# Feed work moved behind a quad's copies, and a stage's last operand pair ahead of its weights

## The reference

```python
x = x + 0.5 * swiglu(rmsnorm(x, ffn1_norm[l]), ...)      # (silu(h @ w_gate) * (h @ w_up)) @ w_down, D_FF = 2816
x = x + mixer(rmsnorm(x, mix_norm[l]))                    # layer 0: gated short convolution, layer 1: attention
x = x + 0.5 * swiglu(rmsnorm(x, ffn2_norm[l]), ...)
...
y = rmsnorm(x, final_norm)
```

## Time and profile before

| | us |
|---|---|
| median of 3 timed runs | 2286.36 (2285.08 to 2289.76) |
| the profiled execution | 2290.18 |
| its span | 2288.4 |
| TensorE busy | 2206.6 |
| VectorE busy | 1372.1 |
| ScalarE busy | 843.4 |
| GpSimd busy | 191.8 |

### The profile page before, as it was taken

One profiled execution on the slowest core, in us unless ns is written; L12 is line 12 of the kernel. 1 busy time (PEld: TensorE's weight loads), 2 busy tenths in 40 slices (PEclk: granted clock), 3 DMA queues, 4 the chain that ended last, 5 costly groups with the idle time before them and its releaser, 6 DMA issues.

```text
span 2288.4 us, 37348 instructions
## 1 busy us (share of the span) xinstructions
PE 2206.6 (96%) x16008; PEld 2132.4 (93%) x16008; DVE 1372.1 (60%) x1861; ACT 843.4 (37%) x1325; POOL 191.8 (8%) x213
## 2 busy tenths in 40 slices
PE   8999999899999999998999999899999999999995
PEld 8999999899899999998999999887787899999995
DVE  6565656755765657467465655855555455756556
ACT  5242424422432434234243332534333332424233
POOL 1000001100110000002000000210000110000002
PEclk9999999999999999999999999999999999999998
DMA  6244343232342343432433342322222142343422
GB/s 195 74 106 116 93 134 97 77 113 83 88 125 79 102 121 87 134 89 69 138 98 112 96 134 74 88 88 74 75 74 75 55 128 82 98 121 87 135 73 75
DMA packets 92917, 226.70 MB, mean 99 GB/s; under 512 B 11024, under 2 KB 25664, under 8 KB 92752
## 3 DMA queue, kind: packets, MB, share of 16 engines
q1 hardware_dynamic: 71712, 186.35, 26.1%
q0 software_dynamic: 17152, 30.26, 7.4%
q10 hardware_dynamic: 3888, 7.70, 0.9%
HBM read 217.17 MB, written 7.09 MB: 98 GB/s over the span
## 4 chain that ended last, share of the span: by engine, by line
PE 86%; DVE 10%; ACT 2%; DMA 1%; issue 1%; POOL 0%; DVEq 0%; ACTq 0%
PE ps L1068 65%; PE ps L1209 15%; DVE w_lo L790 3%; PE ps L1145 2%; PE ps L1127 2%; ACT w_hi L555 1%; DVE xg_lo L803 1%; PE ps L1113 1%; DVE w_quad L797 1%; DVE x L933 1%; DMA w_raw<-w 1%; DVE hop_lo L814 1%; DVE x L928 1%; DVE x L920 1%; DVE w_lo L787 0%
## 5 line engine op out<-in xcount | busy, mean ns | idle before, releaser
L1068 PE MATMUL ps<-xg_hi,w_hi 128*128 128x288 f32 x3584 | 777.2, 298 | 13.2 <-DVE w_lo L787 8.6
L1068 PE MATMUL ps<-xg_hi,w_lo 128*128 128x288 f32 x3584 | 765.4, 295 | 0.0
L1068 PE MATMUL ps<-xg_lo,w_hi 128*128 128x288 f32 x3584 | 764.6, 295 | 0.0
L1068 PEld LDWEIGHTS ps<-xg_hi,w_hi 128*128 128x128 f32 x3584 | 574.5, 189 | 44.8 <-issue 26.5
L1068 PEld LDWEIGHTS ps<-xg_lo,w_hi 128*128 128x128 f32 x3584 | 576.0, 189 | 0.0
L1068 PEld LDWEIGHTS ps<-xg_hi,w_lo 128*128 128x128 f32 x3584 | 575.8, 188 | 0.0
L541 ACT ACTIVATE w_hi<-w_raw 128x1024 fp32r<-128x1024 f32 x232 | 245.3, 1058 | 658.0 <-PE ps L1068 617.1
L1209 PE MATMUL ps<-hop_hi,w_hi 128*128 128x288 f32 x1344 | 406.5, 302 | 47.2 <-ACT snap L694 31.4
L898 DVE TENSOR_TENSOR scaled<-ps,rstd 128x576 f32<-128x576 f32 x176 | 133.1, 757 | 467.1 <-PE ps L1068 466.7
L1209 PE MATMUL ps<-hop_lo,w_hi 128*128 128x288 f32 x1344 | 404.0, 301 | 0.0
L1209 PE MATMUL ps<-hop_hi,w_lo 128*128 128x288 f32 x1344 | 403.3, 300 | 0.0
(11 more groups left out here) (108 smaller groups left out, 1505.9 us busy)
## 6 DMA issues: line engine op xcount, KB each, us to landing
w_raw<-w SPq DMA_DIRECT2D x232, 512.0 KB, 3.5
w_quad<-q SPq DMA_DIRECT2D x180, 256.0 KB, 3.9
w_quad<-q POOLq DMA_DIRECT2D x72, 256.0 KB, 6.1
w_quad<-q SPq DMA_DIRECT2D x80, 192.0 KB, 3.1
w_quad<-q POOLq DMA_DIRECT2D x32, 192.0 KB, 5.0
x<-x_t ACTq DMA_DIRECT2D x8, 288.0 KB, 6.9
k_t<-k_sb ACTq DMA_DIRECT2D x8, 288.0 KB, 2.1
v_t<-v_sb ACTq DMA_DIRECT2D x8, 288.0 KB, 2.5
```

The lines of the kernel that those rows point to most:

```text
L1068: mm = pe.matmul(ps[:, 2 * it.slot + b, 0:HALF], wt[:, r, cols], xt[:, k, b * HALF:(b + 1) * HALF], start=(i == 0 and n == 0), stop=(i == ...
```

## The change

Four things are moved; no arithmetic is added or left out.

1. In a feeding phase ScalarE's and VectorE's feed work of a quad's first tile goes behind the last copy and g4's weights, and that of its second tile into the next quad, behind g1. Only in the phase's last quad (`ends`) the feed work stays where it ends the quad, and `xg_lo` of the first tile goes ahead of line 928.
2. At the last tile of an up phase or of `conv_in`, VectorE rounds the pair (`pair_parts`) ahead of the weights instead of behind them.
3. g4 of a phase's first quad is prepared at the last but one tile, behind g2, instead of at the last one, behind g3; the order of the counted steps follows.
4. `attn_out` calls the same helper `feed`; its order does not change.

GpSimd's sums of squares and all loads stay as they are.

```diff
-        for part in ("g1", "g2", "g3", "g4") if it.phase.quads else ("tile",):
+        if not it.phase.quads:
+            parts = ("tile",)
+        else:
+            parts = ("g1", "g2", "g3", "g4") if it.u else ("g1", "g2", "g4", "g3")
+        for part in parts:
...
-            if nxt is not None and nxt.phase.quads:
-                it.ahead.append(nxt.steps["g4"])
+            if it.u == it.phase.n - 2 and it.phase.after.quads:
+                it.ahead.append(it.phase.after.items[0].steps["g4"])
...
                     act.activation(snap[:, 3, :], ps[:, bank_b, 0:HALF], ACT.Copy).then_inc(snapped, 1)
                     split_hi(g1)
+                    if p.feeds is not None and it.u:
+                        feed(p, before, 1)
                     act.wait_ge(tile_done, it.done + P6)
                     act.activation(snap[:, 1, :], ps[:, bank_a, 0:HALF], ACT.Copy).then_inc(snapped, 1)
                     split_hi(g2)
                     split_hi(g3)
-                    if p.feeds is not None:
-                        act.wait_ge(tile_read, it.evicted + 1)
-                        if p.feeds < N_NORM - 1:
-                            xg_upper(p.feeds, first)
+                    ends = p.feeds is not None and it.u == QUADS - 1
+                    if ends:
+                        feed_upper(p, it, 0)
                     act.wait_ge(tile_done, it.done + P7)
                     act.activation(snap[:, 2, :], ps[:, bank_a, 0:HALF], ACT.Copy).then_inc(snapped, 1)
-                    if p.feeds is not None:
-                        squares(p.feeds, first)
-                        act.wait_ge(tile_read, it.evicted + 2)
-                        if p.feeds < N_NORM - 1:
-                            xg_upper(p.feeds, second)
-                        elif it.u == 0:
-                            act.preload_act_table(ACT.Sqrt)
-                        squares(p.feeds, second)
                     split_hi(g4)
+                    if ends:
+                        squares(p.feeds, 2 * it.u)
+                        feed(p, it, 1)
+                    elif p.feeds is not None:
+                        feed(p, it, 0)
+
+            def feed_upper(p, it, second):
+
+                act.wait_ge(tile_read, it.evicted + 1 + second)
+                if p.feeds < N_NORM - 1:
+                    xg_upper(p.feeds, 2 * it.u + second)
+                elif it.u == 0 and second == 0:
+                    act.preload_act_table(ACT.Sqrt)
+
+            def feed(p, it, second):
+                feed_upper(p, it, second)
+                squares(p.feeds, 2 * it.u + second)
...
+                    last = it.u == p.n - 1
+                    if last:
+                        pair_parts(p, j)
                     if not (p.norm is not None and it.u == 0):
                         for w in it.ahead:
                             split_lo(w)
-                    if it.u % 2:
+                    if it.u % 2 and not last:
                         pair_parts(p, j)
...
                     split_lo(g1)
+                    if p.feeds is not None and it.u:
+                        feed(p, 2 * it.u - 1)
                     split_lo(g2)
...
                     split_lo(g3)
+                    if ends and p.feeds < N_NORM - 1:
+                        norm_lo(p.feeds, 2 * it.u)
                     dve.wait_ge(snapped, shots + 4)
                     dve.scalar_tensor_tensor(halves(x[:, m2, :]), banks(it.slot + 1), -share, halves(x[:, m2, :]),
                                              ALU.mult, ALU.add).then_inc(x_part, 1)
-                    if p.feeds is not None and p.feeds < N_NORM - 1:
-                        norm_lo(p.feeds, 2 * it.u)
                     dve.wait_ge(x_part, 2 * it.quad + 2)
                     dve.scalar_tensor_tensor(halves(x[:, m2, :]), snap[:, 2:4, :], -share, halves(x[:, m2, :]),
                                              ALU.mult, ALU.add).then_inc(tile_read, 1)
-                    if p.feeds is not None and p.feeds < N_NORM - 1:
-                        norm_lo(p.feeds, 2 * it.u + 1)
                     split_lo(g4)
+                    if ends:
+                        feed(p, 2 * it.u + 1)
+                    elif p.feeds is not None:
+                        feed(p, 2 * it.u)
```

More of the change, by code:

```diff
@@ L686, in quads @@
                     g1, g2, g3, g4 = it.ahead
-                    first, second = 2 * it.u, 2 * it.u + 1
                     bank_b, bank_a = 2 * it.slot + 1, 2 * it.slot + 3
@@ L934, in quads, with feed @@
                                              ALU.mult, ALU.add).then_inc(tile_read, 1)
-                    if p.feeds is not None and p.feeds < N_NORM - 1:
-                        norm_lo(p.feeds, 2 * it.u + 1)
                     split_lo(g4)
+                    if ends:
+                        feed(p, 2 * it.u + 1)
+                    elif p.feeds is not None:
+                        feed(p, 2 * it.u)
+            def feed(p, i):
+                if p.feeds < N_NORM - 1:
+                    norm_lo(p.feeds, i)
             def attn_out(p):
@@ L946, in attn_out @@
                         split_lo(w)
-                    norm_lo(p.feeds, it.u)
+                    feed(p, it.u)
             def conv(p):
@@ L991, in conv @@
                             pair_sums(p, jj)
+                            last = it.u == p.n - 1
+                            if last:
+                                pair_parts(p, jj)
                             for w in it.ahead:
                                 split_lo(w)
-                            pair_parts(p, jj)
+                            if not last:
+                                pair_parts(p, jj)
             def qkv(p, t):
```

## The result

The changed kernel takes 2248.1 us (median of 4 runs, 2246.9 to 2249.0), the kernel before 2285.9 us (4 runs, 2285.1 to 2289.8): a ratio of 0.983, interval [0.981, 0.985], 37.8 us less. The forecast was 2238 us, 48.2 us less, in a range of 2217 to 2260. The profiled execution took 2248.87 us with a span of 2247.0; it lies 0.8 us above its median, that of before 4.2 us above its own. Between the two profiles there are 41.3 us.

What follows compares the result with a forecast made beforehand. TensorE, busy 96%, was taken to lose time only to waits, mainly for a VectorE-ScalarE loop in feeding stages, and lowered clock. Waits 36.2 plus clock 12.0 gave 48.2 us off 2286.4: 2238 us, range 2217 to 2260.

Steps and rivals of the forecast that it cites:

- the loop: VectorE and ScalarE work repeated each quad of a feeding stage: 63.0 us to become 53.0, against TensorE's 50.1.
- the waits for `xg_lo`: TensorE's waits, mostly in the next stage's first tile: to grow from 1.0 to near 2.9 us a stage.
- half clock: TensorE at 1.2 instead of 2.4 GHz behind waits: loss to fall from 18.0 to 6.0 us.
- the targeted waits: TensorE's waits for `snap` copies, `hop_lo` and `xg_lo`: 51.8 us to become 15.6, gain 36.2.
- the second turn: Second quad's pass in a feeding stage, from line 933 to line 933: 16.15 us to become 13.2.
- rival C: One more sum holds each turn in feeding stages: 2257 us, chance 0.16; sign: line 933 every 14 us.
- the loads priced at nothing: Loads waiting for g3 start 2.0 us later; block ready at 19 us, wanted at 22.3: no cost.
- Part 2: Stage ends: last pair rounded ahead of the weights, g4 one tile earlier; `hop_lo` waits of 15.8 us fall to 4.0.
- Rival D: Copies late for another reason, loop keeps its 15 us, only stage-start gains come: 2270 us, chance 0.03.
- part 1: Feeding stages: feed work moved behind the copies, taking 2.05 us a turn off ScalarE's chain and 1.8 off VectorE's.
- three-pair starts: Four stage starts: three small waits, about 1.0 us together, instead of 1.76 each; should not lower the clock.
- The first turn: Feeding stage's start to the first line 933's end: 16.1 us to become 15.1.

Runs made afterwards that it cites:

- part 1 alone: Changed kernel with the last pair again rounded behind the weights and g4 back at the last tile, only feed work moved: 2249.6 us.
- g3 between: Changed kernel with the last pair's first part rounded ahead of g3's weights and its second part behind them: 2237.9 us.
- g1 first: Changed kernel with ScalarE rounding the next quad's g1 ahead of the second copy: 2241.1 us.
- small sums: Changed kernel with GpSimd's first sum of squares replaced by a constant fill, the others adding 8 of 576 columns: 2218.3 us.

## Why the prediction was right, and where its size was off

**Right.** The direction, the mechanism and the places. The copies' waits of up to 4.7 us are gone, the loop is what bounds a feeding stage, and the waits for `xg_lo` grew to 2.3 to 2.5 us a stage where 2.9 were forecast, each with a half clock of 3.4 us behind. At the stage starts four waits of 0.4 and four of 0.2 us are left, and the nine with four pairs went. The clock gave 12.2 us where 12.0 were forecast; that all four waits for `xg_lo` lower it is in part luck, since in other kernels two or three of four did.

**Off: the feeding stages' waits.** This is where the size was lost: 22.1 us of the targeted waits are left, not 15.6. In four stages 4 x 2.9 = 11.6 us were forecast; measured are 9.8 for `xg_lo` and 6.4 for copies, 16.2 together. In the fifth stage, whose waits were to go, 1.7 us for copies are left. In the stage shown the loop takes 55.4 us for 53.0, and of the 2.4 us 1.6 lie in the second turn and 0.6 in the third; the second turn, 14.8 us, is past the 14 that the forecast had named as the sign of rival C.

**The first reason: the loads priced at nothing.** The working placed the accumulated block well (it was to land 16.4 us after the stage's start; g1's rounding starts at 388.81 - 371.87 = 16.9, as soon as it is there) but compared it with TensorE's want at 22.3 us. ScalarE comes to g1 in its own list at 387.6, 15.7 us after the start, and what stands behind g1, copies and feed work, waits with it: VectorE stands 1.50 us there, with part 1 alone 0.28. The order that brings the loads earlier took away 6.0 us of waits for copies (9.8 and 3.8), as long as the sums are there; without the sums the late loads cost none in a feeding stage.

**The second reason: sums that were not counted.** In the second turn the two that the forecast counted came (line 939 1.2 us longer, line 952 0.9), and besides them g2's weights and line 810 took 0.2 and 0.3 us longer (393.06 and 394.56). In the third a sum met an `xg_lo`, 1.2 us, besides the one on line 952 that was counted. That is rival C's mechanism at about half its size: some 1.8 us in the stage shown for its 3.2. The Trainium skill's rule (SBUF — State Buffer, "Who interferes with whom"), by which the one that starts first holds the port, had pointed there, and the rows agree: the sum that starts at 395.18 ends at 396.89, and line 939, begun 0.33 us after it, ends 0.61 us behind that. Line 949, which reads PSUM, lies wholly under the sum of 423.53 and takes 0.75 us; line 952 right behind it, with both inputs in SBUF, takes 1.24.

**Part 2 against its forecast.** Rival D has 15.8 - 4.0 + 4.5 = 16.3 us for it beside an unchanged loop; alone it brought 6.3. Beside part 1 the forecast's own loop gives it less. Without part 2 TensorE comes 0.97 us later into four feeding stages, which leaves 4 x 1.93 = 7.7 us of waits there and 15.8 at the starts: part 1 alone is then worth 51.8 - 23.5 = 28.3 us in waits and 18.0 - 6.0 - 4.5 = 7.5 in clock, together 35.8, and part 2 on top of it 12.4. Measured are 36.4 and 1.5. That the first agrees is luck: with part 1 alone 28.4 us of waits are left, 4.9 more, and three stretches at half clock instead of seven. On top of part 1, part 2 took away 6.3 us of waits (28.4 to 22.1) where 7.9 were forecast; with it came two half clocks more, where three fewer were forecast.

**Small.** The three-pair starts cost 4.2 us against 4.0: 1.7 + 0.8, and 1.65 of waits for copies (0.55 + 0.28 + 0.28 + 0.54) that were not there before. The first turn by its own terms is 16.1 - 0.9 = 15.2, not 15.1, and 15.2 was measured. And 3.4 us of the gap between 48.2 and 37.8 come from working with one profiled execution that stood further above its median before than after.

**Open.** Why a wait lowers the clock in one run and not in the next: the four `xg_lo` waits of 2.3 to 2.5 us did so four times in the changed kernel, twice with part 1 alone, twice with g3 between, three times with g1 first; the four waits of 1.76 us at stage starts did so three times before and once with part 1 alone, and the `hid_lo` wait of 1.66 us in some of the kernels and not in others. No run here was made to tell it.

## What to carry to other kernels

A transfer that comes later is late when the first engine that uses it reaches it in its own list, not when the last consumer wants the result; with lists in fixed order, everything behind it waits, and whether that costs time depends on what else fills the turn. A small operation on an idle engine isn't free: here a sum of 1.4 us on GpSimd made an instruction of VectorE up to 1.2 us longer. Look for rows of the same instruction with two durations, and try the work on the engine that it disturbs. Once a wait is removed, put the loop's turn beside TensorE's work per turn, since the difference decides whether the next edit pays.

## What was not expected of the hardware

- VectorE's busy time fell from 1371.2 us in the changed kernel to 1362.8 with the sums on VectorE, although it took over 34 additions (25.5 us) and 5 copies (2.3 us). So these 39 had held it up by some 36 us while GpSimd did them, a third more than VectorE needs for the work itself. With small sums its busy time is 1341.0 us, 30.2 less than in the changed kernel.
- The disturbance goes both ways. A sum takes 1.42 us where it starts just ahead of VectorE's instruction (412.38, line 952 at 412.45 then takes 1.96), and the one at 404.63, begun 0.02 us behind VectorE's line 810, takes 1.97 us, with an `xg_lo` of 2.00 us from 405.22 on.
- The price of GpSimd's sums isn't a property of the sums: leaving them out gave 30 us in one order of the same work and 10 us in another, where other edits had already taken the waits.
